# Final norm of a two-layer decoder trunk: the last two output tiles are worked chunk by chunk, and the norm, the turns and the stores of finished blocks stand between the projections

## The reference, cut to what matters

```python
def rmsnorm(x, g):
    r = lax.rsqrt(jnp.mean(xf * xf, axis=-1, keepdims=True) + EPS)
    return (xf * r).astype(x.dtype) * g

# end of each layer, in branch_output
    x = x + mix @ w_out
    return x + jax.nn.sigmoid(x @ w_pg) * (p_i @ w_pp)
...
y_prompt = rmsnorm(xp, g_final)
y_sample = rmsnorm(xs, g_final)
```

## Time and profile before

| what | value |
|---|---|
| median of 3 runs | 1226.89 us (1225.06 to 1227.0) |
| span of the profiled execution | 1226.8 us, the time that the trace covers from its first to its last instruction |
| PE busy | 1187.1 us (97% of the span) |
| weight loads busy | 1129.9 us (92%) |
| DVE busy | 739.2 us (60%) |
| ACT busy | 424.5 us (35%) |
| mean granted PE clock | 0.986 |
| last slot's sigmoid starts | 1206.78 us |
| first store of y issued | 1213.96 us |

### The profile page before, as it was taken

How to read it: one execution, slowest core, us unless ns; L and a number is a source line. 1 busy time by engine, 2 the same in 40 slices (tenths; PEclk the granted TensorE clock), 3 DMA queues, 4 the chain that set the end, 5 groups by cost and what they waited for, 6 DMA issues and landing times.

```text
span 1226.8 us, 18225 instructions
## 1 busy us (share of the span) xinstructions
PE 1187.1 (97%) x7302; PEld 1129.9 (92%) x7302; DVE 739.2 (60%) x1286; ACT 424.5 (35%) x919; POOL 319.0 (26%) x149
## 2 busy tenths in 40 slices
PE   5999899999999999999999989999999999999997
PEld 5999888888899999999999988887889999999997
DVE  2356879798535444466623587988945454444554
ACT  5311545445233222333321044454522332223333
POOL 2324321222222221221322432222122312221110
PEclk9999899999999999999999999999999999999998
DMA  7533101110121122111053311110111122121103
GB/s 210 147 84 87 34 21 32 35 35 20 41 44 58 52 53 61 43 44 53 26 155 88 87 36 35 35 31 28 30 35 35 42 69 69 41 65 44 44 1 142
DMA packets 127946, 70.40 MB, mean 57 GB/s; under 512 B 43156, under 2 KB 123860, under 8 KB 127832
## 3 DMA queue, kind: packets, MB, share of 16 engines
q1 hardware_dynamic: 122400, 61.33, 17.6%
q10 hardware_dynamic: 5464, 7.92, 2.6%
HBM read 59.10 MB, written 6.76 MB: 54 GB/s over the span
## 4 chain that ended last, share of the span: by engine, by line
PE 83%; DVE 12%; ACT 2%; DMA 1%; issue 1%; ACTq 0%; DVEq 0%
PE ring L399 73%; PE aux L422 2%; DVE yc L1063 2%; PE aux L455 2%; DVE up L1059 2%; PE aux L444 1%; PE aux L457 1%; DVE yc L1061 1%; DMA xnat<-in_x_prompt_dram 1%; DVE st L953 1%; PE aux L430 1%; DVE comb L1032 1%; DVE st L1034 1%; DVE tmp L983 0%; ACT comb L757 0%
## 5 line engine op out<-in xcount | busy, mean ns | idle before, releaser
L399 PE MATMUL ring<-act,ws 128*128 128x352 f32 x6048 | 995.6, 324 | 0.5 <-DVE rot L978 0.3
L399 PEld LDWEIGHTS ring<-act,ws 128*128 128x128 f32 x6048 | 974.1, 189 | 1.6 <-DVE act L891 0.5
L375 POOL TENSOR_TENSOR ws<-stage,ws 128x1024 fp32r<-128x1024 f32 (+1 forms) x84 | 212.0, 2524 | 841.5 <-ACT ws L629 841.5
L638 ACT ACTIVATE act<-tmp 128x352 fp32r<-128x352 f32 x120 | 59.6, 497 | 278.2 <-DVE tmp L1097 143.6
L629 ACT ACTIVATE ws<-stage 128x1024 fp32r<-128x1024 f32 (+1 forms) x84 | 91.5, 1089 | 110.5 <-issue 61.3
L371 POOL TENSOR_TENSOR stage<-stage,gT 128x1024 f32<-128x1024 f32 x52 | 107.3, 2064 | 24.3 <-DMA stage<-in_w_in_dram 13.4
L884 DVE TENSOR_TENSOR act<-tmp,act 128x352 fp32r<-128x352 f32 x120 | 73.6, 614 | 60.3 <-ACT act L638 59.5
L1117 DVE TENSOR_TENSOR tmp<-ring,gate 128x352 f32<-128x352 f32 x48 | 25.2, 524 | 75.0 <-ACT gate L816 75.0
L1095 DVE TENSOR_TENSOR tmp<-ring,act 128x352 f32<-128x352 f32 x48 | 25.2, 524 | 63.4 <-PE ring L399 63.4
L757 ACT ACTIVATE comb<-comb,st 128x128 f32<-128x128 f32 x128 | 49.9, 391 | 32.0 <-DVE st L1040 31.9
L722 ACT ACTIVATE gate<-gate 128x352 f32<-128x352 f32 x48 | 23.8, 496 | 101.8 <-DVE gate L985 76.3
(11 more groups left out here) (167 smaller groups left out, 930.0 us busy)
## 6 DMA issues: line engine op xcount, KB each, us to landing
stage<-in_w_in_dram SPq DMA_DIRECT2D x36, 512.0 KB, 3.9
stage<-in_w_in_dram SPq DMA_DIRECT2D x32, 256.0 KB, 3.8
stage<-in_w_pg_dram SPq DMA_DIRECT2D x16, 512.0 KB, 3.8
rot<-raw ACTq DMA_DIRECT2D x32, 132.0 KB, 2.3
stage<-in_w_out_dram SPq DMA_DIRECT2D x32, 128.0 KB, 2.8
stage<-in_w_out_dram SPq DMA_DIRECT2D x16, 256.0 KB, 3.1
out_dram<-xnat SPq DMA_DIRECT2D x8, 512.0 KB, 2.9
xnat<-in_x_prompt_dram SPq DMA_DIRECT2D x4, 512.0 KB, 7.1
```

The costliest lines, as they stand in the source:

```text
L375: nc.gpsimd.tensor_tensor(ws[:, s, 1, 0:n, :], stage[:, s, 0:n, :], ws[:, s, 0, 0:n, :].bitcast(F32), ALU.subtract).then_inc(w_lo, 1)
L399: mm = nc.tensor.matmul(out, ws[:, w % 2, wp, kw, :], x[:, xp, kx, cs], start=(i == 0 and wp == 0 and xp == 0), stop=(i == n - 1 and wp == 1))
L638: nc.scalar.activation(dst, tmp[:, s % 2, :], ACT.Copy).then_inc(S["hi_out"], 1)
```

## The change

In the last layer slots 18 to 23 go through tiles 6 and 7 chunk by chunk: (6, 0), (7, 0), (6, 1), (7, 1), (6, 2), (7, 2) (`out_tile`). A block of which all chunks are complete can then be normed while later slots run. Blocks are handled in three parts (0 and 1; 2 to 4; 5 to 8) and turned by halves (4 of the 8 feature tiles, 256 KB), 18 units in the order of `Y_UNITS` (block, half, bank). The sums of part 0 and units 0 to 2 stand on PE after slot 20, the sums of part 1 and units 3 to 5 after slot 22, the rest after slot 23. Even units are evicted by DVE, odd ones by ACT, in the orders of `Y_ORDER`; each unit has a store of its own. The squares of slot 23 are no longer added by DVE: PE sums them with a second matmul. In the last layer DVE adds the two parts of the residual ahead of the product. The output is collected in another part of SBUF (`ynat`).

```diff
+    def out_tile(l, s):
+        if l < DEPTH - 1 or s < (KT - 2) * NCH:
+            return divmod(s, NCH)
+        c, i = divmod(s - (KT - 2) * NCH, 2)
+        return KT - 2 + i, c
+    def out_before(l, s):
+        f, c = out_tile(l, s)
+        return [i for i in range(s) if out_tile(l, i)[1] == c][-1] if f else None
+    def squares_in(l, s):
+        return l * NSQ + s - NCH + 1
+    PARTS = ((0, 2), (2, 5), (5, NB + 1))
+    Y_UNITS = ((0, 0, 0), (0, 1, 1), (1, 0, 2), (1, 1, 0), (2, 0, 1), (2, 1, 2),
+               (3, 0, 3), (3, 1, 4), (4, 0, 0), (5, 0, 5), (6, 0, 6), (4, 1, 1), (7, 0, 2), (8, 0, 3),
+               (5, 1, 4), (6, 1, 0), (7, 1, 5), (8, 1, 6))
+    Y_ORDER = (tuple(range(0, 18, 2)), (1, 3, 5, 7, 11, 9, 13, 15, 17))
+    def y_engine(i):
+        return i % 2, Y_ORDER[i % 2].index(i) + 1
...
+                ynat, _ = place("ynat", [P, NB, D], F32, lo)
...
-        y_turns = [pS] + [ring[:, i:i + 2, :].rearrange("p a n -> p (a n)") for i in (0, 2)]
-        FIRST = 5
+        y_banks = [aux[:, i, :] for i in range(3)] + [ring[:, i, :] for i in range(4)]
...
# SP
-            for b in range(NB + 1):
-                sp.wait_ge(y_ready[b % 2], b // 2 + 1)
+            for i, (b, h, _) in enumerate(Y_UNITS):
+                e, n = y_engine(i)
+                sp.wait_ge(y_ready[e], n)
+                half = slice(h * 4 * P, (h + 1) * 4 * P)
                 if b < NB:
-                    sp.dma_start(y_prompt[0, b * P:(b + 1) * P, :], xnat[:, b, :]).then_inc(S["y_out"], 16)
+                    sp.dma_start(y_prompt[0, b * P:(b + 1) * P, half], y_place(b, h)).then_inc(S["y_out"], 16)
...
# PE
+            def y_sums(part):
+                last = (KT - 2) * NCH + 2 * part + 1
+                if part < NCH - 1:
+                    pe.wait_ge(S["acc_done"], squares_in(DEPTH - 1, last))
+                else:
+                    pe.wait_ge(S["acc_done"], squares_in(DEPTH - 1, last - 1))
+                    pe.wait_ge(S["sq_out"], DEPTH * B_SLOTS)
+                for b in range(*PARTS[part]):
...
+                    mm = nc.tensor.matmul(pO[:, b:b + 1], acc[:, t0:t0 + P], ones[:, 0:1], start=True, stop=not more,
+                                          skip_group_check=True)
+                    if more:
+                        mm = nc.tensor.matmul(pO[z0 - t0:P, b:b + 1], yc[:, z0:t0 + P], ones[:, 0:1], start=False,
+                                              stop=True, skip_group_check=True)
+                mm.then_inc(S["ss_done"], 1)
+            def turn_y(i):
+                b, h, at = Y_UNITS[i]
+                t0 = b * P if b < NB else LASTB
+                before = [j for j in range(i) if Y_UNITS[j][2] == at]
+                if before:
+                    e, n = y_engine(before[-1])
+                    pe.wait_ge(y_ready[e], n)
+                elif at >= 3:
+                    pe.wait_ge(free[at - 3], uses(at - 3, DEPTH * GROUPS))
+                if h:
+                    last = (KT - 2) * NCH + 2 * min(NCH - 1, (t0 + P - 1) // CH) + 1
+                    pe.wait_ge(S["y_scaled"], last + 1)
+                else:
+                    pe.wait_ge(S["y_scaled"], 4 * NCH)
+                for k in range(4):
+                    mm = nc.tensor.transpose(y_banks[at][:, k * P:(k + 1) * P], xfin[:, 4 * h + k, t0:t0 + P], ident[:])
+                mm.then_inc(S["y_turned"], 1)
...
-                for f in range(KT):
+                for s in range(B_SLOTS):
+                    f, c = out_tile(l, s)
                     w = l * FT + NA + KT + f
                     pe.wait_ge(w_lo, w + 1)
...
+                    if l == DEPTH - 1:
+                        if s == B_SLOTS - 4:
+                            y_sums(0)
+                            for i in range(3):
+                                turn_y(i)
+                        elif s == B_SLOTS - 2:
+                            y_sums(1)
+                            for i in range(3, 6):
+                                turn_y(i)
+            for i in range(6, 12):
+                turn_y(i)
+            y_sums(2)
+            for i in range(12, len(Y_UNITS)):
+                turn_y(i)
# ACT
+            def y_root(part):
+                bs = slice(*PARTS[part])
+                sc.wait_ge(S["mean_done"], DEPTH + 1 + part)
+                nc.scalar.activation(nr[:, 1, bs], nr[:, 0, bs], ACT.Sqrt).then_inc(S["root_done"], 1)
+            def y_evict(i):
+                b, h, at = Y_UNITS[i]
+                sc.wait_ge(S["y_turned"], i + 1)
+                sc.wait_ge(S["r_done"], y_part(i) + 1)
+                nc.scalar.activation(y_place(b, h), y_banks[at], ACT.Copy, scale=nr[:, 5, b:b + 1]).then_inc(y_ready[1], 1)
...
                 for s in range(B_SLOTS):
-                    f, c = s // NCH, s % NCH
+                    f, c = out_tile(l, s)
                     w = l * FT + NA + KT + f
                     if c == 0 and w + 1 < DEPTH * FT:
                         split_weights(w + 1)
...
+                    if l == DEPTH - 1 and s == B_SLOTS - 1:
+                        y_root(1)
...
+                        if s == B_SLOTS - 3:
+                            y_root(0)
+                        elif s == B_SLOTS - 2:
+                            y_evict(1)
...
+            for i in Y_ORDER[1][1:5]:
+                y_evict(i)
+            y_root(2)
+            for i in Y_ORDER[1][5:]:
+                y_evict(i)
# DVE, slot loop
+                    if l == DEPTH - 1 and s == B_SLOTS - 3:
+                        y_mean(0)
+                    if l == DEPTH - 1 and s == B_SLOTS - 1:
+                        y_mean(1)
...
-                        V.tensor_tensor(xfin[:, f, cols(c)], t, xa[:, 1, f, cols(c)].bitcast(F32), ALU.add)\
-                         .then_inc(S["out_split"], 1)
+                        x = xfin[:, f, cols(c)]
+                        link(V.tensor_tensor(x, xa[:, 0, f, cols(c)].bitcast(F32), xa[:, 1, f, cols(c)].bitcast(F32), ALU.add))
+                        ve.wait_ge(free[(g + 1) % 4], uses((g + 1) % 4, g + 2))
+                        V.tensor_tensor(t, src, gate[:, s % 2, :], ALU.mult).then_inc(free[g % 4], 1)
+                        ve.wait_ge(free[g % 4], uses(g % 4, g + 1))
+                        V.tensor_tensor(x, x, t, ALU.add).then_inc(S["out_split"], 1)
+                    if l == DEPTH - 1:
+                        if s == B_SLOTS - 3:
+                            norm_scale(DEPTH, slice(*PARTS[0]))
+                            y_evict(0)
+                        elif s == B_SLOTS - 2:
+                            y_evict(2)
...
+            norm_scale(DEPTH + 1, slice(*PARTS[1]))
+            for i in range(4, 9, 2):
+                y_evict(i)
+            y_mean(2)
+            norm_scale(DEPTH + 2, slice(*PARTS[2]))
+            for i in range(10, len(Y_UNITS), 2):
+                y_evict(i)
```

## The result

The changed kernel takes 1236.69 us, median of 4 runs (1235.09 to 1240.03), and the kernel before 1226.34 in the same job (1225.06 to 1227.0): a ratio of 1.0094 (95%: 1.0075 to 1.0112), slower. A second run of the changed kernel in a later job gave 1237.89 and 1.0101 (1.0086 to 1.0115).

What follows compares the result with a forecast made beforehand. PE, busy 46.70 of 46.70 us in the last ten slots, was taken as the bound; only the tail could shrink. 2.35 + 3.7 + 2.0 + 2.15 + 1.7 - 3.2 = +8.7 on 1226.8 gave 1235.6, range 1230.5 to 1239.5.

Steps and rivals of the forecast that it cites:

- Step 1: Before slot 19: PE waits for tile 7's late weights, finished by POOL; +2.35 us.
- Step 2: Between the projections: sums and turns of parts 0 and 1 cost their PE time; +3.7 us.
- Step 3: Before slot 23: part 1's sums wait for slot 21's squares, added behind part 0's root and unit 0's eviction; +2.0 us.
- Step 4: Before slot 23: unit 4's turn waits for ACT's eviction of unit 1 from the same bank; +2.15 us.
- Step 5: Slow clock behind PE's idle stretches: one slow stretch, under slot 23; +1.7 us, bounds 0 to 3.5.
- Step 6: Tail behind slot 23: shorter than the 20.0 us before, by 3.2 us, between 3.8 and 2.0.
- What would show it: List of expected signs, among them 5.9 us from slot 22's end to slot 23's start, with two idle stretches of PE.
- slot 22 not holding PE: Rival: additions and eviction come in time before slot 23; +2.3 to +2.9, 1229.1 to 1229.7; chance 0.10.
- none of the waits lasting: Rival: weights and banks are free before PE asks; 1226.7, or 1224.9 if stores run unbroken; chance 0.08.
- a tail that does not shrink: Rival: the stretch behind slot 23 gets no shorter; chance 0.12.
- a load that holds ACT for twice its row: Rival: each table load costs ACT 1.28 us more, before slot 23 and in the tail; +2.6, 1238.2; chance 0.02.

Runs made afterwards that it cites:

- the third buffer: Changed kernel, but tile 7's weights are split into a third buffer at slot 16, two slots earlier: 1234.36, ratio 1.0071.
- the turns later: Changed kernel, but units 3 to 5 are turned after slot 23, the sums of part 1 staying in place: 1233.09, ratio 1.0066.
- Squares first: Changed kernel, but DVE adds slot 21's squares before part 0's scale and unit 0's eviction: 1238.75, ratio 1.0106.
- after again: The changed kernel run once more without edits, in a later job: 1237.89, ratio 1.0101.
- Filling the waits: Changed kernel, but PE fills all three waits with unneeded turns (20, 16, and unit 3 turned five times): 1234.39, ratio 1.0066, against 1237.89 unfilled in the same job.
- the kernel of the three edits: Changed kernel with third weight buffer, squares added before the eviction, and units 3 to 5 turned after slot 23: 1226.84, ratio 0.9999.
- the kernel of part 2 early: The kernel of the three edits, but part 2's sums follow unit 7's turn and its root comes one eviction sooner: 1225.44, ratio 0.9996.
- the tiles in order: Tile 6 then tile 7 as before the change; only part 0's sums and units 0 to 2 between slots 22 and 23: 1226.26, ratio 1.0002.
- the two kernels after it: On the tiles in order: all turns behind slot 23 (1228.73, ratio 1.0030); then also seven banks and part 2's sums behind the seventh unit (1224.55, ratio 0.9998).
- the kernel that fills the first wait alone: Changed kernel, but PE does 20 turns into an unused bank before slot 19 while weights arrive: 1238.77, ratio 1.0106.

## Why the prediction was right, step by step

Slower, by 1236.69 against 1235.6 predicted: the three waits and the work stood where they were put, within 0.3 us each. Two terms were mis-sized.

That the medians lie only 1.1 from the forecast is in part luck. Both terms were off to the same side, and in the profiled execution, the longest of four, the terms come to 13.65 - 1.5 = 12.15, 3.4 above the forecast and just inside its upper bound of 12.4. In the later job the two medians lie 12.6 apart (1237.89 and 1225.28).

- **Step 1, weights:** 1184.35 - 1182.08 = 2.27, predicted 2.35. Shown by the third buffer, which removes it.
- **Step 2, added work:** sums and turns of part 0 take 1197.20 - 1195.58 = 1.62. Those of part 1 ran partly at the slow clock (0.63 granted from 1209 to 1210, 0.50 behind it); at full clock the sums took 1206.46 - 1205.77 = 0.69 with the turns later, and three turns take 1197.20 - 1195.94 = 1.26, as in part 0. Together 3.57, predicted 3.7.
- **Step 3, squares behind the root:** 1208.70 - (1202.06 + 4.77) = 1.87, predicted 2.0. Squares first removes it, and shows that it costs only 0.4 on its own, because step 4 waits for later work.
- **Step 4, unit 1's eviction:** unit 3's turn begins at 1209.51, and at its price of 0.45 unit 4's could begin at 1209.96. It began at 1211.83: 1.87, predicted 2.15. The profile counts 1.23 of it as idle and the rest as unit 3's turn, which took 1.09; in after again that turn ran at full clock in 0.63, and 1.81 counts as idle. ACT did not stand idle behind the root's load here either: the load of 1.28 us began at 1204.94, the root at 1206.23.
- **Step 5, the clock, mis-sized:** 13.65 less steps 1 to 4 (2.27, 3.57, 1.87, 1.87) leaves 4.1, predicted 1.7. I took one slow stretch, under slot 23, with two as the bound. There were two: 1.7 under slot 19, 1.3 under slot 23 and about 1 in the sums and turns between. Filling the waits gives 3.2 for it, measured on the chip. What was wrong was the choice among: behind one gap of 2.8 us there the clock fell (0.79) and behind one it did not (1.00), and I let the wait of 2.3 before slot 19 go as the second. The trace of before has three more such gaps, 3.09, 2.80 and 2.80 us long (PE goes on at 731.16, 789.13 and 859.93), and the clock fell behind each: 0.83 from 726 to 736, 0.81 from 785 to 794, 0.83 from 856 to 866. So it had fallen behind four gaps of that length and not behind one. In the slot behind this wait the clock fell in all four profiles that leave the wait unfilled: slot 18's stretch is 8.74 and 8.77 in the two of after, 8.75 with squares first, 8.73 with the turns later, with 0.80 to 0.81 granted over each of these stretches.
- **Step 6, the tail, mis-sized in the first profile:** -1.5, predicted -3.2 between -3.8 and -2.0; -3.1 in the second. Unit 8's turn waited for unit 3 until 3.47 after zero (predicted 3.65), but turns 8 to 11 ran at the slow clock (0.50 granted from 1223 to 1226) to 1226.5, 6.8 after zero against 5.5, and part 2's scale was ready at 10.1 against 8.8. With the clock up, the estimate holds: -2.9 in the kernel of the three edits. The clock splits the tails of all eight profiles that have part 2's sums behind unit 11 in two: 18.5 to 18.7, and 19.64 with the waits filled, where the first 10 us had 0.83, and 16.8 to 17.1 where they had 1.00. The lower bound of the term, 2.0 won, did not reach the slow case.
- **The start:** I set the profiled span of 1226.8 equal to the median of before. About 1.7 us lie around a span (1225.08 and 1223.3, 1240.03 and 1238.3), so that execution took some 1228.5, longer than the median of its runs. As the sum was in effect laid on the median, this moved the forecast by nothing. Between the spans lie 11.5, between the medians 10.35, and 8.7 was predicted.
- **A slip in the working:** from slot 22's end to slot 23's start, steps 2 to 4 give 2.0 + 0.62 + 1.35 + 2.15 = 6.1, not the 5.9 under "What would show it"; 6.62 was measured. The sum of the forecast does not use it.

Of the rivals, slot 22 not holding PE is refuted by the waits of 1.71 and 1.23, and the second, none of the waits lasting, is what the kernel of the three edits does: it was priced at 1226.7 (3.7 of work, 3.8 off the tail) and came to 1226.84 (2.46, with three turns fewer, and 2.9). The third, a tail that does not shrink, is refuted by 18.5 and 17.06 against 20.0. The fourth, a load that holds ACT for twice its row, is refuted by the load of 1.28 between its neighbours (step 4).

**Open.** Slots 17 to 22 and the tail together are 2.3 us shorter in the kernel of part 2 early (46.3 against 48.6) and 1.4 in that of seven banks (47.2), and neither ratio shows it; 2.3 would be a ratio of 0.998, below the interval of the first (0.9987 to 1.0005), while 1.4 lies at the edge of the second's. The time up to slot 17 moves by more than this between executions of one kernel, so it can hide there; whether something takes it back always, no run tells.

## What to carry to other kernels

Work put between the instructions of a full engine costs its time and, above all, what it waits for (here 3.57 us of work and 6.0 of waits): follow each wait through the in-order lists of the other engines (here a root behind a scaling, an addition behind an eviction), and for each bank name who must empty it first. Removing the earlier of two waits in a row gives almost nothing while the later one stands (0.09 us at slot 23's zero here). Where idle stretches fall into a dense run of matmuls, price the slow clock behind each one as likely (here it fell behind the 2.3 us before slot 19 in four profiles of four, and in the kernel of late turns not behind 1.7 us), and check it by filling the gap with idle work before redesigning the order.

## What was not expected of the hardware

PE idled 2.1 us before slot 19 and ran below full clock behind it (0.81 over 4.3 us; slot 19 took 6.46 there and 6.48 in the second profile), while 1.7 us of idling in the kernel of late turns was followed by none (1.00 over 7.5 us). Making PE work more (36 more transposes and a turn four times over) made the kernel 3.5 us faster. In the kernel that fills the first wait alone, 20 of them cost next to nothing: that stretch took 7.17 - 4.77 = 2.40 more than a plain slot, against the wait of 2.27.

A table load does not always start as soon as ACT is free, as I took it from the earlier trace rows, where it stood at 1210.02 with DVE's mean still running. With the tiles in order, the load for part 1's root began at 1210.77, after 1.27 us of idling and 0.07 behind the end of DVE's mean (1210.54 and 0.16); so it was in the two kernels after it (1.33 of idling, 0.09 and 0.08). In these traces ACT had stood idle before the late loads, and had just ended an operation, 0.02 us earlier, before those that began while the mean ran. Whether this is what tells the two cases apart was not tried.
